# Full matmuls of one projection placed between the small input matmuls of a state space layer, on one Trainium2 core

## The reference

```
h = x @ ab_w_in[j]
out_a = s5_mixer(h[..., :D_A], ...)      # state space layer on u, the first 512 features
out_b = pool_mixer(h[..., D_A:], ...)    # sliding means on v, the other 512 features
mix = concatenate([out_a, out_b]) @ ab_w_out[j]
```

```
bu_re = einsum('bsgh,gph->sbgp', u32, bb_re)      # the input of the states, and bu_im likewise
_, _, st_re, st_im = associative_scan(...)        # state = a * state + bu, over the 256 tokens
y = einsum(st_re, c_re) - einsum(st_im, c_im) + d_skip * u32
out = gelu(y) * sigmoid(gelu(y) @ w_glu)
```

## Time and profile before

| | |
|---|---|
| Time, median of 3 runs | 1304.94 us (1304.3 to 1305.15) |
| Span of the profiled execution | 1306.6 us |
| PE busy | 1245.4 us, 95% |
| PEld busy | 898.2 us, 69% |
| DVE busy | 607.8 us, 47% |
| ACT busy | 473.4 us, 36% |
| POOL busy | 206.1 us, 16% |
| Chain that ended last | PE 87%, DMA 6%, DVE 4%, ACT 2% |
| Mean granted TensorE clock | 0.985 |

### The profile page before, as it was taken

How to read it: one execution, slowest core, us unless ns; L and a number is a source line. 1 busy time by engine, 2 the same in 40 slices (tenths; PEclk the granted TensorE clock), 3 DMA queues, 4 the chain that set the end, 5 groups by cost and what they waited for, 6 DMA issues and landing times.

```text
span 1306.6 us, 17981 instructions
## 1 busy us (share of the span) xinstructions
PE 1245.4 (95%) x7640; PEld 898.2 (69%) x7640; DVE 607.8 (47%) x814; ACT 473.4 (36%) x643; POOL 206.1 (16%) x207
## 2 busy tenths in 40 slices
PE   7999999999999999999899999987999899999985
PEld 6999997887799999889673434334898684343332
DVE  6645446855676665556661111105467661111103
ACT  5543444556445444324330111114477441111101
POOL 0000000320399992021000000000033100000000
PEclk9999999999999999979899999998999999999998
DMA  9555553541455555413689999999532579999994
GB/s 383 197 179 190 192 174 136 184 152 65 169 192 175 182 194 185 177 65 119 246 336 388 423 421 421 421 418 389 189 110 98 204 289 389 424 420 421 421 420 198
DMA packets 49045, 338.32 MB, mean 259 GB/s; under 512 B 5440, under 2 KB 5440, under 8 KB 10176
## 3 DMA queue, kind: packets, MB, share of 16 engines
q1 hardware_dynamic: 47232, 330.53, 65.6%
q10 hardware_dynamic: 1728, 6.55, 1.3%
HBM read 336.02 MB, written 1.05 MB: 258 GB/s over the span
## 4 chain that ended last, share of the span: by engine, by line
PE 87%; DMA 6%; DVE 4%; ACT 2%; issue 1%; SPq 0%; ACTq 0%; DVEq 0%
PE pb L179 85%; DMA ring<-in_moe_w 4%; DMA XN<-in_ln_b 1%; DMA ring<-in_ffn_w 1%; DVE Xs L1540 1%; DVE halves L309 1%; DVE Xs L412 0%; PE pb L1994 0%; ACT halves L301 0%; PE pb L373 0%; DVE XN L349 0%; DVE Xs L414 0%; DVE Xs L1535 0%; DVE p L1700 0%; DVE SM L1516 0%
## 5 line engine op out<-in xcount | busy, mean ns | idle before, releaser
L309 DVE TENSOR_TENSOR halves<-ring,halves 128x2048 fp32r<-128x2048 f32 (+1 forms) x122 | 285.3, 2354 | 130.8 <-ACT halves L301 130.5
L179 PE MATMUL pb<-XTh,halves 128*128 128x256 f32 x1856 | 338.7, 283 | 5.6 <-DVE XTl L401 3.6
L179 PEld LDWEIGHTS pb<-XTh,halves 128*128 128x128 f32 x1856 | 291.2, 192 | 8.6 <-issue 4.1
L179 PE MATMUL pb<-XTl,halves 128*128 128x256 f32 x928 | 262.3, 283 | 0.0
L301 ACT CAST halves<-ring 128x2048 fp32r<-128x2048 f32 (+1 forms) x122 | 227.7, 1873 | 81.3 <-PE pb L179 75.7
L179 PE MATMUL pb<-ring,gather 128*64 128x512 f32 x784 | 178.2, 596 | 1.8 <-DMA ring<-in_moe_w 1.8
L179 PEld LDWEIGHTS pb<-XTl,halves 128*128 128x128 f32 x928 | 177.8, 192 | 0.9
L179 PE MATMUL pb<-halves,XTh 128*128 128x512 f32 x512 | 160.1, 394 | 0.7 <-DVE XTl L396 0.7
L179 PEld LDWEIGHTS pb<-ring,gather 128*64 128x64 f32 x784 | 54.5, 137 | 102.2 <-issue 101.5
L2127 DVE TENSOR_TENSOR slots_h<-slots_silu,pb 128x256 f32<-128x256 f32 x32 | 13.5, 422 | 236.7 <-ACT slots_silu L2089 236.7
L179 PE MATMUL pb<-halves,HTh 128*128 128x512 f32 x352 | 110.8, 396 | 0.0
(11 more groups left out here) (357 smaller groups left out, 1440.3 us busy)
## 6 DMA issues: line engine op xcount, KB each, us to landing
ring<-in_moe_w SPq DMA_DIRECT2D x140, 1024.0 KB, 16.3
ring<-in_ffn_w SPq DMA_DIRECT2D x66, 1024.0 KB, 4.9
extra<-in_moe_w SPq DMA_DIRECT2D x44, 1024.0 KB, 15.5
ring<-in_w_tok SPq DMA_DIRECT2D x10, 1024.0 KB, 4.9
ring<-in_ple_gate SPq DMA_DIRECT2D x8, 1024.0 KB, 4.8
ring<-in_w_out SPq DMA_DIRECT2D x4, 1024.0 KB, 4.9
ring<-in_ab_out SPq DMA_DIRECT2D x4, 1024.0 KB, 5.0
ring<-in_moe_w SPq DMA_DIRECT2D x8, 512.0 KB, 25.9
```

Source lines behind the costliest of these rows:

```text
L179: return e.matmul(out, l, r, start=start, stop=stop, **kw)
L309: e.tensor_tensor(l, raw_of(n), h.bitcast(F32), ALU.subtract).then_inc(*low.mark(n))
```

## The change

`pe_inputs` now takes one quarter `q`, and TensorE's wait for `in_kept` moves in front of the first quarter. The projection v is no longer done by `pe_tok` but by a new function `pe_v(half, t, ks)`, which does the chunks `ks` of one weight block and one token tile. Behind quarter `q` of the inputs now stands chunk `k = q` of the first weight block for the first token tile: three matmuls of 512 columns into bank 0. The other 36 matmuls of the projection follow behind `pe_recent` in the order they had. No matmul is added or removed, and no other engine's program is changed. `x_done` stands on the last matmul of the fourth quarter, behind nine of the moved matmuls.

```
-        def pe_inputs(e):
-            e.wait_ge(*in_kept.at(1))
-            for q in range(4):
-                for x in range(2):
...
+        def pe_inputs(e, q):
+            for x in range(2):
+                for n in range(4):
+                    for a_ in range(4):
...
+            if q == 3:
+                i.then_inc(*x_done.mark())
+
+        def pe_v(e, half, t, ks):
+            blk, W = weights(e, ("ab_v", half), k=4)
+            for k in ks:
+                i = mm3(e, banks[t][:, :], both(XT3, lambda x: x[:, 4 * half + k, t * 128:t * 128 + 128]),
+                        both(W, lambda x: x[:, k, :]), half == 0 and k == 0, half == 1 and k == 3)
+            if k == 3 and t == 1:
+                i.then_inc(*used.mark(blk))
+            elif k == 3 and half == 1:
+                i.then_inc(*half_done.mark("ab_v"))
...
         def pe_ssm(e):
             pe_proj(e, ("ab_u", 0), XT3, banks[0], "ssm")
             pe_proj(e, ("ab_u", 1), XT3, banks[1])
-            pe_inputs(e)
+            e.wait_ge(*in_kept.at(1))
+            for q in range(4):
+                pe_inputs(e, q)
+                pe_v(e, 0, 0, (q,))
             pe_recent(e)
-            pe_tok(e, "ab_v", 0, 1)
+            pe_v(e, 0, 1, range(4))
+            for t in range(2):
+                pe_v(e, 1, t, range(4))
             pe_windows(e)
```

More of the change, by code:

```diff
@@ L1272, in pe_recent @@
             i.then_inc(*recent_done.mark())
-        def pe_inputs(e):
-            e.wait_ge(*in_kept.at(1))
-            for q in range(4):
-                for x in range(2):
[L1278 to L1282, removed]
+        def pe_inputs(e, q):
+            for x in range(2):
+                for n in range(4):
+                    for a_ in range(4):
+                        r, o_ = slice(32 * a_, 32 * a_ + 32), x * 256 + q * 64
+                        i = mm(e, banks[4 + a_][:, o_:o_ + 64], BK[3 - n][x][r, q, :], u4[r, q, :, n], n == 0, n == 3)
+            if q == 3:
[9 more added lines that the diff above has]
+                i.then_inc(*half_done.mark("ab_v"))
         def pe_direct(e, q):
```

## The result

| | before | after |
|---|---|---|
| Median of 12 runs on one chip | 1302.25 us | 1307.11 us |
| Lowest to highest | 1299.86 to 1305.15 | 1304.79 to 1312.7 |
| Profiled execution, span | 1306.6 us | 1310.8 us |
| The same execution, time | not given | 1312.7 us |
| Mean granted clock | 0.985 | 0.983 |

The ratio after to before is 1.0046, 95% interval 1.0034 to 1.0058: 0.46% slower, some 6 us. (The ratio is not the quotient of the two medians, which is 1.0037; the same holds for the ratios further down.) The forecast was no change.

The account below looks back on a forecast made before the run. It took TensorE to bound the stage, with VectorE 0.8 us behind. A gain of 2.2 us less 1.7 us for a clock fall gave 0.5 us off 1304.94, so 1304.4 us; range 1302.0 to 1309.3.

Parts of the forecast that it names:

- The baseline: Difference worked out against the first profile's 1306.6 us span, with 13.6 us at half clock, then taken off 1304.94 us.
- x_done is 1.3 us earlier: End of the inputs: last matmul starts at 567.6 us against 568.8, clock held; bounds 0.3 and 2.0 us.
- The likeliest case: Clock holds in the inputs, falls in the new stop: 2.2 - 1.7 = 0.5 us gained, 1304.4 us; chance 0.42.
- A: Rival: the clock also outlives the new stop at the fourth pe_direct; 2.2 us gained, 1302.7 us; chance 0.26.
- VectorE as the next bound: At the fourth pe_direct: VectorE's fourth turn (L1415) is only 0.8 us behind being the bound.
- The gain of 2.2 us: TensorE ends v 6.0 us earlier but resumes at the fourth pe_direct at 589.3 instead of 591.56; bounds 1.2 and 2.9.
- the small wait: VectorE's wait for the recent kernel at 572.91 us, 0.21 us, was to go.
- The changes of shape: Six steps between matmul shapes on TensorE ahead of x_done, 0.10 us each, 0.6 us together.
- The wait for the weight block: Each moved group waits on TensorE for the low part of its weight block; costed at nothing.
- The new stop and the fall behind it: TensorE waits 3.7 us at the fourth pe_direct, then the clock falls, losing 1.7 us.
- Rival B: The clock falls in the inputs all the same; x_done near 574.4, TensorE 4.3 us late, 1309.2 us; chance 0.26.

Follow-up runs that it names:

- before_again: The kernel before, unchanged, run for a second profile: 1304.25 us, span 1302.4 us.
- the filled pair: The kernel before and the changed kernel, each with two unused full matmuls in TensorE's wait ahead of the inputs: 1303.39 and 1308.99 us.
- relieved_after: The changed kernel with the recent kernel moved ahead of the inputs, its VectorE copy and one weight split ahead of x_done: 1301.61 us, ratio 0.9999.
- one_group: `relieved_after` with one group of three matmuls, behind the second quarter, instead of three groups ahead of x_done: 1299.80 us, ratio 0.9978 to before.
- early: The kernel before with the recent kernel's matmuls moved ahead of the inputs and VectorE's copy of it ahead of its first unit: 1304.01 us, ratio 0.9996.
- early_split: `early` with one VectorE weight split also moved ahead of its wait for x_done: 1303.05 us, ratio 1.0006 to before.
- six: The changed kernel with six full matmuls of v behind each quarter instead of three, of both token tiles: 1309.43 us, ratio 1.0040 to before.
- filled_after: The changed kernel with two unused full matmuls in TensorE's wait ahead of the inputs: 1308.99 us, ratio 1.0044 to before.
- filled_stop: `filled_after` with six more unused full matmuls ahead of the fourth pe_direct: 1307.85 us, ratio 1.0036 to before.
- twelve: The changed kernel with twelve full matmuls of v behind each quarter, so all of v precedes the recent kernel: 1314.22 us, ratio 1.0070 to before.
- filled_before: The kernel before with two unused full matmuls in TensorE's wait ahead of the inputs: 1303.39 us, ratio 0.9998.
- split_early: The kernel before with one VectorE weight split moved ahead of its wait for x_done: 1303.48 us, ratio 1.0010.
- behind: The changed kernel with its four groups in one piece behind the fourth quarter, ahead of the recent kernel: 1306.74 us, ratio 1.0022 to before.
- before_third: The kernel before, unchanged, run for a third profile: 1305.59 us.
- after_again: The changed kernel, unchanged, run for a second profile: 1312.54 us.
- after_third: The changed kernel, unchanged, run for a third profile: 1314.1 us.

## Why the prediction was wrong

**The baseline (failed, and it decided the outcome).** "I work out a difference against the span and take it off the median." The difference was worked out against an execution that had lost the clock in the inputs, 6 us longer than the median. In most executions that loss isn't there: `before_again` held the clock, and VectorE started 3.8 us earlier; by their mean clock some three quarters of before's runs seem to have held it too. The failed step is "x_done is 1.3 us earlier". Its comparison with the last start at 568.8 counts a loss of clock that the usual execution does not have. With the clock held in both kernels `x_done` is 3.3 us later (the filled pair), and where the clock fell it is 5.85 us later than in the first profile. The likeliest case and A have it earlier.

**VectorE as the next bound (right in kind, its slack wrong).** The limit stands in the chain after, and the fourth `pe_direct` waits for the line that was named. But it wasn't 0.8 us behind being the bound: with the clock held it already was, by 1.2 us. Any delay of `x_done` thus reached TensorE at once. The gain of 2.2 us, which is x_done's 1.3, the 0.2 of the small wait and the 0.8 of slack, has no part left with the clock held.

**The changes of shape (mis-sized).** Taken at 0.10 us each, bounds 0 and 0.28; they measured 0.2 at 2.4 GHz. Six of them cost 1.2 of the 3.3 us, the groups themselves 2.0. The Trainium skill says in TensorEngine Tiling (Array Packing), section "Key Properties", that changing the tiling mode drains the engine; the trace agrees in so far as each change costs time.

**The wait for the weight block (right).** No stop stands at the moved groups in any profile.

**The new stop and the fall behind it (right in kind).** Forecast 3.7 us, measured 2.34 to 3.03, with a fall in three of the four profiles (not in after's first); the forecast price of the fall, 1.7 us, measured 1.57 and 1.68. The likeliest case named these parts, but set them against a gain of 2.2 us that wasn't to be had. (It puts the fall's lowest price at 0 in one place and at 0.5 us in its range.)

**Rival B (right for the executions profiled, underpriced).** The clock fell in the inputs in all three profiles of after. B gave 574.4 for `x_done` (its own terms, 560.5 + 10.9 + 2.7 + 0.8, make 574.9) and 4.3 us for TensorE's delay; measured were 575.10 and 6.63. The term it lacked is VectorE's wait for the recent kernel: 32 matmuls at half clock behind one group, 1.77 us. The prediction had that wait go, which is right only with the clock held.

**The chances.** Slower had 0.24, and all of it was B. The case that the filled pair shows, slower with the clock held, was not among the rivals. It would have come out of one question to the rows: what if the first profile's clock isn't the usual one? That the measured time lies within the stated range is B's doing and no merit of the likeliest case.

What stays open: why the clock falls in the inputs in one execution and not in another, and how often exactly, since the mean clock of a run does not say where it fell. For the same reason the 0.46% can't be split into clock and VectorE for after itself, only for the filled pair: 3.7 us late start (0.4 of it not the change's), 1.6 us the fall behind the stop.

## What to carry to other kernels

Where a profile shows a clock fall without a long stop ahead of it, take a second profile before counting it as something to win, hold the first one's span against the median of more than three runs, and its mean clock against theirs. Work that is placed ahead of a signal delays everybody who waits for it by its whole length and its changes of shape, so find the waiting engine's slack first, with the clock as it mostly is. If that slack is gone, relieve the waiting engine first (`relieved_after`); placing less work there (`one_group`) gave the best time of all, though the runs do not tell it from `relieved_after`.

## What the runs showed of the hardware

- The same row of small matmuls (32 rows of contraction) kept 2.4 GHz for 7.8 us in one execution and dropped to 1.2 GHz after 2.9 and 2.7 us in two others, with PE busy throughout in all three. In `early` and `early_split` it dropped after 6.6 and 7.2 us. The Trainium skill's TensorE: Matmul & The Clock Gate, section "What's actually happening", says of the change to full clock that its moment varies from run to run; the traces show the like for the fall, and here it varies whether the fall comes at all.
- Whether full matmuls among the small ones help to keep the clock is not shown. With groups it held through the inputs in one profile each of `six`, `filled_after`, `filled_stop`, `relieved_after` and `one_group`, and fell in all three of after and in `twelve`; without groups it held in `before_again`, `filled_before`, `split_early` and `behind`, and fell in `before`, `before_third`, `early` and `early_split`. Once down, single groups did not bring it back at once (17.1 to 20.5 us in after's profiles), the twelve full matmuls in a row of `twelve` had it back after 3.4 us.
- Stops of 2.34 to 3.03 us were each followed by 3.4 us at 1.2 GHz, in `behind`, `after_again`, `after_third` and `filled_after`, but not in after's first profile, where the stop was 2.34 too. With the stops of 4.32 and 4.67 us in `six` and `twelve` it was 6.8 us. Stops of 1.2 us were not followed by one, nor was the 3.23 us stop of the earlier trace rows. The fall of 3.4 us cost 1.57 to 1.68 us.
- A change between matmuls of 32 x 128 and 128 x 128 costs 0.2 us at 2.4 GHz (`filled_after` against `filled_before`).
